# When the dense matrix of the second token tile is built: six units in it instead of seven, and an issue ratio of five gathers to four

## Chip, core and metric

The kernel runs on one core of a Trainium2 chip. The metric is the device time of one execution in microseconds (us); lower is better. Three runs of the kernel before gave 1784.56, 1786.32 and 1787.67 us, median 1786.32.

## What is computed

A decoder layer over 256 tokens of width 2048: attention and gated convolution, an output projection, a layer norm giving h, then a retrieval of single-neuron experts (PEER), then a second layer norm. The change lies wholly in PEER:

```python
q = (h @ w_query).reshape(B, S, 8, 2, 128)
s = einsum('bshcd,hckd->bshck', q, sub_keys)      # two lists of 128 keys per head
# top 16 of each list, top 16 of the 16x16 sums; eid = i1 * 128 + i2
g = softmax(best_s)
a = gelu(einsum('td,thkd->thk', h, expert_u[eid]))
y = einsum('thk,thkd->td', g * a, expert_v[eid])
```

Each of 256 tokens picks 16 experts in each of 8 heads out of 16384. Each pick reads one row of `expert_u` and one of `expert_v`, 2048 float32 each (8 KB).

## The kernel before

**Tiles and units.** The tokens form tile 0 and tile 1 of 128 tokens, one token per partition. A unit is one tile and one head: units 0 to 7 are tile 0, units 8 to 15 are tile 1. A unit has 16 picks, numbered m = 16 n + k. One indirect DMA of the GpSimd (POOL) queue brings one pick of all 128 tokens, a 128 x 2048 tile of 1 MB: `gather_u` (L525) into one of 8 `u_slot`s, `gather_v` (L542, L545) into one of 7 `v_slot`s.

**Four steps per pick.** (1) VectorE (DVE) multiplies the U rows by the tokens and sums (`dot`, L1760). (2) ScalarE (ACT) takes exp and gelu per unit (`unit`, made of `expo_gate` and `gelu_unit`), and DVE makes the coefficients (`gates_of`, L1766 to L1771, which counts `coef_ok`). (3) For V picks 0 to 143 TensorE (PE) adds the V rows, times diagonal matrices that ACT writes (`diagonals`), into PSUM (L974). (4) For V picks 144 to 255 DVE adds them into `xh` (`add_row`, L1795) after its last dot and after one scaling of `xh` (L1839).

**The dense part.** The last 40 x 128 = 5120 rows of `expert_v` (first key index 88 or more) are not gathered for units that use `bounds_check=ROWS - 1`: a pick in them moves nothing, and its coefficient in `gate` is made zero. They are instead multiplied as a dense product at the end: for each of 40 blocks f, 128 rows of `expert_v` are loaded by the SP queue (L429) into `u_slot` f % 6 and multiplied with a 128 x 128 coefficient matrix of tile 0 and one of tile 1 (`dense_mm`, L946, 8 matmuls issued as 2 passes each of 128 x 512 for each tile and block; tile 1 runs three blocks behind tile 0). The last unit, 15, is gathered whole (L545) and stands in no matrix.

**Building the matrix.** Per tile: PE transposes the ids and coefficients of its units (`pick_transposes`, L928; `PICKS` is the number of rows, 128 for tile 0 and 112 = 7 units for tile 1), ACT copies them (`picks_out`, L1307). Then for 16 groups b of 8 tokens: DVE makes two one-hot tables (`hot_rows`, L1783, L1785, L1788), PE multiplies them (`dense_rows`, L938, 16 passes), ACT copies the result into `dense0` or `dense1` (`dense_out`, L1316; L1319 and L1320). There are two buffers, so `hot_rows` b waits for `dense_rows` b - 2, and `dense_rows` b for `dense_out` b - 2.

**What sets the order.** Every engine's queue is written out by hand. POOL sends V picks in order and before V pick m as many U picks as `64 + (m + 1) * 4 // 3` (L555); at m = 144 all U picks left. A U gather waits for the dot eight before it, a V gather for the pick seven before it to be used. DVE's queue is the 256 dots; `HOT0_AT` and `HOT1_AT` say after which dot a `hot_rows` of tile 0 or 1 stands (192 to 233 for tile 0; 244 to 254 for groups 0 to 7 of tile 1, groups 8 to 15 behind the last dot). `gates_of(n - 1)` stands at k = 10 of unit n, for the last one at k = 2. PE's queue is V picks 0 to 143 with `dense_rows` of tile 0 before picks 97, 99, ... 127, the token tile's own product (L963) before pick 128, `pick_transposes(1)` before pick 132 and `dense_rows` of tile 1 groups 0 to 7 before picks 133 to 140, groups 8 to 15 behind pick 143, then `sum0` (L981) and the 40 blocks. SP's first six block loads wait for dots 248 to 253, the others for PE (`dense_used`). DVE takes the statistics of tile 0 before V pick 246, writes tile 0's result before pick 248 and adds PE's sum of tile 1 before pick 253 (L1847 to L1859).

Of the kernel before, what the change touches and what calls it, by code (L numbers as in the profile page):

```python
# [12 lines left out]
P = 128  # L13
# [15 lines left out]
NKEY = 128  # L29
TOPK = 16  # L30
NU = 16
RU = 8
RV = 7
AHEAD = 4
EARLY_V = 4
PH = 8
V0_PICKS = TOPK * PH
PE_PICKS = V0_PICKS + TOPK
RD = 6
FD = 40  # L40
FA = 24
ROWS = (NKEY - FD) * NKEY
LEAD = 3
G_TOK = 8
NG_T = P // G_TOK
PICKS = (P, P - TOPK)
IDS_AT = {(0, 4): 1, (8, 9): 10, (9, 1): 11, (9, 9): 12, (10, 1): 13, (10, 9): 14, (11, 1): 15}
IDS_AT.update({(n, 1): n + 1 for n in range(1, 9)})
HOT0_AT = {12 * TOPK + 11 * b // 4: b for b in range(NG_T)}
HOT1_AT = {15 * TOPK + 4 + 3 * b // 2: b for b in range(NG_T // 2)}  # L50
HTW = SEQ + 2
TCOL = (slice(0, P), slice(P + 2, SEQ + 2))
JOBS = [(0, (0,)), (1, (0,)), (0, (1,)), (1, (1,))] + [(h, (0, 1)) for h in range(2, PH)]
# [69 lines left out]
def build(nc, x, w_in, cmp_k_pos, cmp_k_w1, cmp_k_b1, cmp_k_w2, cmp_v_pos, cmp_v_w1, cmp_v_b1, cmp_v_w2,  # L123
# [133 lines left out]
    b_id = at("b_id", [P, 2, NU, TOPK], F32, o_lo + 2 * K)  # L257
    u_dot = at("u_dot", [P, NU, TOPK], F32, o_lo + 4 * K)
    gate = at("gate", [P, NU, TOPK], F32, o_lo + 5 * K)
# [182 lines left out]
    def _(pool):  # L442
# [86 lines left out]
        def gather_v(n, k):  # L529

            m = TOPK * n + k
            if m == 0:
                pool.wait_ge(S["wq_used"], 12)
            if m == EARLY_V:
                pool.wait_ge(S["wq_used"], 16)
            if RV <= m < PE_PICKS + RV:
                pool.wait_ge(S["v_used"], m - RV + 1)
            if m >= PE_PICKS + RV:
                pool.wait_ge(S["v_dve"], m - RV - PE_PICKS + 1)
            src = bass.IndirectOffsetOnAxis(ap=eid[:, n, k:k + 1], axis=0)  # L540
            if n < NU - 1:
                nc.gpsimd.indirect_dma_start(out=v_slot[m % RV][:, :], out_offset=None, in_=expert_v[0], in_offset=src,  # L542
                                             bounds_check=ROWS - 1, oob_is_err=False).then_inc(s_v[m % RV], 16)
            else:
                nc.gpsimd.indirect_dma_start(out=v_slot[m % RV][:, :], out_offset=None, in_=expert_v[0], in_offset=src  # L545
                                             ).then_inc(s_v[m % RV], 16)
# [5 lines left out]
                    gather_v(0, k)  # L552
        sent = TOPK * AHEAD
        for m in range(EARLY_V, TOPK * NU):
            while sent < min(TOPK * NU, TOPK * AHEAD + (m + 1) * 4 // 3):  # L555
                gather_u(sent // TOPK, sent % TOPK)
                sent += 1
            if m == PE_PICKS:
                while sent < TOPK * NU:
                    gather_u(sent // TOPK, sent % TOPK)  # L560
                    sent += 1
            gather_v(m // TOPK, m % TOPK)
# [3 lines left out]
    def _(pe):  # L566
# [354 lines left out]
        scores_of(len(JOBS) - 1)  # L921
        def pick_transposes(t):

            pe.wait_ge(S["coef_ok"], (PH, NU - 1)[t])
            n = PICKS[t]
            units = slice(PH * t, PH * t + n // TOPK)
            for i, src in enumerate((b_id[:, 0, units, :], b_id[:, 1, units, :], b_val[:, units, :])):
                ins = nc.tensor.transpose(bank[(2, 6)[t]][0:n, P * i:P * i + P], src.rearrange("p n k -> p (n k)"), ident[:, :])  # L928
            ins.then_inc(S["pick_mm"], 1)

        def dense_rows(t, b):

            g, n = NG_T * t + b, PICKS[t]
            pe.wait_ge(S["hot_ok"], g + 1)
            if g >= 2:
                pe.wait_ge(S["dense_ok"], g - 1)
            for i in range(G_TOK):
                ins = nc.tensor.matmul(bank[4 * t + g % 2][:, FD * i:FD * i + FD], hot2[0:n, g % 2, i, :], hot1[0:n, g % 2, i, :],  # L938
                                       start=True, stop=True, skip_group_check=True)
            ins.then_inc(S["dense_mm"], 1)  # L940
# [12 lines left out]
        for m in range(PE_PICKS):  # L953
            n, k = divmod(m, TOPK)
            if k == 0:
                pe.wait_ge(S["diag_ok"], n + 1)
            if m == 80:
                pick_transposes(0)
            if m >= 97 and m % 2 and m < V0_PICKS:
                dense_rows(0, (m - 97) // 2)  # L960
            if m == V0_PICKS:
                for q in range(4):
                    ins = nc.tensor.matmul(bank[4 + q][:, :], ident_a[:, :], xh[:, 0, 512 * q:512 * q + 512],  # L963
                                           start=False, stop=True)
                ins.then_inc(S["t0_part"], 1)
                pe.wait_ge(S["dense_ok"], NG_T)
            if m == V0_PICKS + 4:
                pe.wait_ge(S["part_ok"], 1)
                pick_transposes(1)
            if V0_PICKS + 5 <= m < V0_PICKS + 5 + NG_T // 2:  # L970
                dense_rows(1, m - V0_PICKS - 5)
            pe.wait_ge(s_v[m % RV], 16 * (m // RV + 1))
            for q in range(4):
                ins = nc.tensor.matmul(bank[(4 if n < PH else 0) + q][:, :], diag[:, n % 2, k, :],  # L974
                                       v_slot[m % RV][:, 512 * q:512 * q + 512], start=(m in (0, V0_PICKS)), stop=False)
            ins.then_inc(S["v_used"], 1)
        for b in range(NG_T // 2, NG_T):
            dense_rows(1, b)
        pe.wait_ge(S["dense_ok"], 2 * NG_T)
        for q in range(4):  # L980
# [10 lines left out]
    def _(act):  # L991
# [280 lines left out]
        def gelu_unit(n):  # L1272
            act.wait_ge(S["dots_done"], TOPK * (n + 1))
            nc.scalar.activation(u_dot[:, n, :], u_dot[:, n, :], ACT.Gelu_apprx_tanh).then_inc(S["gelu_ok"], 1)

        def diagonals(n):
            act.wait_ge(S["coef_ok"], n + 1)
            if n >= 2:
                act.wait_ge(S["v_used"], TOPK * (n - 1))
            for k in range(TOPK):  # L1280
                ins = nc.scalar.activation(diag[:, n % 2, k, :], ident[:, :], ACT.Copy, scale=gate[:, n, k:k + 1])
            ins.then_inc(S["diag_ok"], 1)
# [21 lines left out]
        def picks_out(t):  # L1304
            act.wait_ge(S["pick_mm"], t + 1)
            n = PICKS[t]
            nc.scalar.activation(pickT[0:n, t, :, :].rearrange("p a t -> p (a t)"), bank[(2, 6)[t]][0:n, 0:3 * P], ACT.Copy  # L1307
                                 ).then_inc(S["pick_ok"], 1)
# [14 lines left out]
        def unit(n):  # L1323
            expo_gate(n)
            gelu_unit(n)
# [13 lines left out]
        diagonals(5)  # L1339
        unit(9)  # L1340
        diagonals(6)
        unit(10)
        picks_out(0)
        unit(11)
        diagonals(7)
        for b in range(NG_T):
            if b in (6, 12):
                unit(11 + b // 6)
            if b == 10:
                diagonals(8)  # L1350
            dense_out(0, b)
        act.wait_ge(S["t0_part"], 1)
        for q in range(4):
            ins = nc.scalar.activation(sum0[:, 512 * q:512 * q + 512], bank[4 + q][:, :], ACT.Copy)
        ins.then_inc(S["part_ok"], 1)
        unit(14)
        expo_gate(15)
        picks_out(1)
        for b in range(NG_T):
            if b == NG_T // 2:  # L1360
                gelu_unit(15)
            dense_out(1, b)
        for t in range(2):
            root(t)

# [2 lines left out]
    def _(dve):  # L1368
# [394 lines left out]
        def gates_of(n):  # L1763

            dve.wait_ge(S["exp_ok"], n + 1)
            V.reciprocal(g_inv[:, n:n + 1], g_sum[:, n:n + 1])  # L1766
            dve.wait_ge(S["gelu_ok"], n + 1)
            dve.drain()
            V.scalar_tensor_tensor(b_val[:, n, :], u_dot[:, n, :], g_inv[:, n:n + 1], b_val[:, n, :], ALU.mult, ALU.mult)
            dve.drain()  # L1770
            V.scalar_tensor_tensor(gate[:, n, :], b_id[:, 0, n, :], float(NKEY - FD) if n < NU - 1 else float(NKEY),  # L1771
                                   b_val[:, n, :], ALU.is_lt, ALU.mult).then_inc(S["coef_ok"], 1)

        def hot_rows(t, b):
# [40 lines left out]
        for n in range(NU):  # L1815
            for k in range(TOPK):
                dot(n, k)
                if (n, k) == (0, 1):
                    dve.wait_ge(S["t1_mm"], 4)
                    last_row(1)  # L1820
                    mean_of(1)
                if (n, k) in IDS_AT:
                    ids(IDS_AT[n, k])
                if (n, k) == (0, 8):
                    inverse_std(1)
                    dve.wait_ge(S["yt_mm"], 9)
                    for half in range(2):
                        token_major(1, half)
                    dve.drain().then_inc(S["h1_ok"], 1)
                if n and k == (10 if n < NU - 1 else 2):  # L1830
                    gates_of(n - 1)
                m = TOPK * n + k
                if m in HOT0_AT:
                    hot_rows(0, HOT0_AT[m])
                if m in HOT1_AT:
                    hot_rows(1, HOT1_AT[m])
        for b in range(NG_T // 2, NG_T):
            hot_rows(1, b)
        V.tensor_scalar(xh[:, 1, :], xh[:, 1, :], ALPHA, None, ALU.mult)  # L1839
        dve.drain()  # L1840
# [56 lines left out]
```

## Time and profile before

| | us |
|---|---|
| median of three runs | 1786.32 |
| the profiled execution, its own time | 1785.23 |
| its span, first to last instruction | 1783.5 |
| PE busy | 1515.2 (85%) |
| DVE busy | 1361.8 (76%) |
| POOL busy | 963.2 (54%) |
| ACT busy | 391.1 (22%) |

The sixteen DMA engines are near 100% busy from about 45% of the span on, but for a hole in slices 31 and 32 of 40. Times in the rows count from the span's start. A row of the stretches gives for each engine the busy time and number of instructions, then the granted TensorE clock as a share of 2.4 GHz, the busy share of the DMA engines and their GB/s.

### The profile page before, as it was taken

Reading aid. Unit: us, or ns where it says so; the run is one execution under the profiler, and the core shown is the slowest. Engines: PE = TensorE matmul, PEld = TensorE weight load, DVE = VectorE, ACT = ScalarE, POOL = GpSimd, SP = SyncE. Lnnn points to the kernel's source line nnn. Section 1 sums busy time; section 2 is a strip of 40 time slices with the busy share of each in tenths; the row PEclk is TensorE's granted clock in tenths of the full one; section 3 lists DMA queues with packets and bytes.
Section 4 is the critical chain, followed back from the end, with each engine's and each line's share of the span. In section 5 each row is a group of like instructions: output and inputs, shape, how many; then the busy total and the mean of one; then the engine's idle time right before and its main releaser. Section 6 shows DMA issues by size and latency. Waiting matters only on the chain.

```text
span 1783.5 us, 16886 instructions
## 1 busy us (share of the span) xinstructions
PE 1515.2 (85%) x6164; PEld 950.5 (53%) x6164; DVE 1361.8 (76%) x1915; ACT 391.1 (22%) x824; POOL 963.2 (54%) x591
## 2 busy tenths in 40 slices
PE   8999999999989709888777778798977899999970
PEld 7988999988668504333333333344534564444430
DVE  6666646676879998776788888677867487788788
ACT  5665464664101211102010110101210110000000
POOL 3210000000456677878776767888886147578761
PEclk9999999999989859898999988999997879999995
DMA  9876444474999999999999999999999639999994
GB/s 313 288 257 198 120 141 142 143 250 162 377 380 421 389 425 418 420 425 426 420 425 425 417 425 418 422 420 412 415 406 418 235 118 401 405 404 408 414 414 179
DMA packets 159380, 610.87 MB, mean 343 GB/s; under 512 B 21467, under 2 KB 74807, under 8 KB 97255
## 3 DMA queue, kind: packets, MB, share of 16 engines
q0 software_dynamic: 79232, 480.80, 66.2%
q1 hardware_dynamic: 80064, 128.99, 20.3%
q8 instruction: 48, 0.79, 0.2%
q14 instruction: 36, 0.29, 0.0%
HBM read 683.42 MB, written 2.10 MB: 384 GB/s over the span
## 4 chain that ended last, share of the span: by engine, by line
PE 33%; DMA 22%; DVE 18%; POOL 15%; issue 9%; DVEq 2%; ACT 1%; SPq 0%; POOLq 0%; ACTq 0%
PE psum_all L587 13%; DMA v_slot<-in_expert_v_dram,eid 13%; POOL v_slot L542 9%; DVE u_slot L1760 8%; DMA u_slot<-in_expert_u_dram,eid 8%; PE psum_all L974 7%; POOL u_slot L525 6%; PE psum_all L727 4%; DVE xh L1795 3%; PE psum_all L938 2%; PE psum_all L752 1%; PE psum_all L708 1%; PE psum_all L612 1%; PE psum_all L614 1%; PE psum_all L674 0%
## 5 line engine op out<-in xcount | busy, mean ns | idle before, releaser
L974 PE MATMUL psum_all<-v_slot,diag 128*128 128x512 f32 x1152 | 570.9, 650 | 152.6 <-DMA v_slot<-in_expert_v_dram,eid 104.4
L1760 DVE SCALAR_TENSOR_TENSOR u_slot<-u_slot,xh 128x2048 f32<-128x2048 f32 x256 | 577.7, 2289 | 149.6 <-DMA u_slot<-in_expert_u_dram,eid 148.4
L525 POOL DMA_INDIRECT u_slot<-in_expert_u_dram,eid x256 | 445.4, 1740 | 267.1 <-DVE u_slot L1760 99.7
L542 POOL DMA_INDIRECT v_slot<-in_expert_v_dram,eid x240 | 452.8, 1887 | 176.1 <-issue 63.6
L974 PEld LDWEIGHTS psum_all<-v_slot,diag 128*128 128x128 f32 x1152 | 231.7, 208 | 471.5 <-issue 271.0
L1795 DVE SCALAR_TENSOR_TENSOR xh<-v_slot,gate,xh 128x2048 f32<-128x2048 f32 x112 | 263.5, 2353 | 52.5 <-DMA v_slot<-in_expert_v_dram,eid 44.5
L1378 DVE TENSOR_TENSOR w_lo<-w_ring,w_hi 128x512 fp32r<-128x512 f32 x240 | 156.6, 688 | 77.6 <-ACT w_hi L1010 74.5
L587 PE MATMUL psum_all<-act_hi,w_hi 128*128 128x256 f32 x640 | 185.0, 289 | 1.2 <-DVE w_lo L1378 1.2
L587 PE MATMUL psum_all<-act_lo,w_hi 128*128 128x256 f32 x640 | 180.8, 282 | 0.0
L587 PE MATMUL psum_all<-act_hi,w_lo 128*128 128x256 f32 x640 | 180.2, 282 | 0.0
L1010 ACT ACTIVATE w_hi<-w_ring 128x512 fp32r<-128x512 f32 x240 | 139.3, 622 | 42.3 <-PE psum_all L587 41.2
L946 PE MATMUL psum_all<-u_slot,dense 128*128 128x512 f32 x320 | 143.4, 592 | 0.0
L587 PEld LDWEIGHTS psum_all<-act_hi,w_hi 128*128 128x128 f32 x640 | 121.2, 189 | 13.7 <-issue 4.1
L752 PE MATMUL psum_all<-hT,wq_ring 128*128 128x258 f32 (+2 forms) x640 | 120.8, 349 | 8.6 <-DMA wq_ring<-in_w_query_dram 8.2
L587 PEld LDWEIGHTS psum_all<-act_lo,w_hi 128*128 128x128 f32 x640 | 121.2, 189 | 2.7 <-issue 0.5
L587 PEld LDWEIGHTS psum_all<-act_hi,w_lo 128*128 128x128 f32 x640 | 121.0, 189 | 0.0
L752 PEld LDWEIGHTS psum_all<-hT,wq_ring 128*128 128x128 f32 x640 | 106.0, 198 | 24.0 <-DMA wq_ring<-in_w_query_dram 8.6
L513 POOL DMA_DIRECT2D skeys<-in_sub_keys_dram x1 | 1.2, 1165 | 197.1 <-PE psum_all L587 197.1
L946 PEld LDWEIGHTS psum_all<-u_slot,dense 128*128 128x128 f32 x320 | 60.8, 190 | 76.5 <-issue 76.5
L938 PEld LDWEIGHTS psum_all<-hot,hot 128*128 128x128 f32 (+1 forms) x512 | 76.0, 233 | 29.6 <-DVE hot L1788 20.7
L938 PE MATMUL psum_all<-hot,hot 128*128 128x40 f32 (+1 forms) x512 | 75.5, 318 | 15.7 <-DVE hot L1788 15.7
L946 PE MATMUL psum_all<-u_slot,dense1a 128*128 128x512 f32 x192 | 86.3, 592 | 0.0
(283 smaller groups left out, 1462.7 us busy)
## 6 DMA issues: line engine op xcount, KB each, us to landing
w_ring<-in_w_in_dram SPq DMA_DIRECT2D x88, 512.0 KB, 5.0
u_slot<-in_expert_v_dram SPq DMA_DIRECT2D x40, 1024.0 KB, 8.7
wo_ring<-in_w_out_dram SPq DMA_DIRECT2D x32, 512.0 KB, 5.0
wq_ring<-in_w_query_dram SPq DMA_DIRECT2D x32, 512.0 KB, 10.0
w_ring<-in_cmp_k_w_dram POOLq DMA_DIRECT2D x16, 512.0 KB, 6.0
w_ring<-in_cmp_v_w_dram POOLq DMA_DIRECT2D x16, 512.0 KB, 4.4
u_slot<-in_expert_u_dram,eid POOLq DMA_INDIRECT x256
v_slot<-in_expert_v_dram,eid POOLq DMA_INDIRECT x256
```

What stands on the lines that cost most here:

```text
L525: nc.gpsimd.indirect_dma_start(out=u_slot[m % RU][:, :], out_offset=None, in_=expert_u[0], in_offset=bass.IndirectOffsetOnAxis(ap=eid[:, n ...
L542: nc.gpsimd.indirect_dma_start(out=v_slot[m % RV][:, :], out_offset=None, in_=expert_v[0], in_offset=src, bounds_check=ROWS - 1, oob_is_er ...
L587: ins = nc.tensor.matmul(o, st, mv, start=(k == 0 and b == 0 and i == 0), stop=(k == KC - 1 and i == 2), skip_group_check=True)
L727: ins = nc.tensor.matmul(bank[acc + b][:, :], st[:, k, half], mv[:, n % RING, :], start=(i == 0 and m == 0), stop=(i == KC - 1 and m == 2))
L752: ins = nc.tensor.matmul(bank[QBANK[h % 2] + c][:, cols], wq_ring[j % 2][:, k // 4, k % 4, 256 * (h % 2) + 128 * c:256 * (h % 2) + 128 * c ...
L938: ins = nc.tensor.matmul(bank[4 * t + g % 2][:, FD * i:FD * i + FD], hot2[0:n, g % 2, i, :], hot1[0:n, g % 2, i, :], start=True, stop=True ...
L946: ins = nc.tensor.matmul(bank[(4 if t == 0 else 0) + q][:, :], src, u_slot[f % RD][:, 512 * q:512 * q + 512], start=False, stop=(f == FD - 1))
L974: ins = nc.tensor.matmul(bank[(4 if n < PH else 0) + q][:, :], diag[:, n % 2, k, :], v_slot[m % RV][:, 512 * q:512 * q + 512], start=(m in ...
L1010: nc.scalar.activation(w_hi[:, n % RING, :], raw_item(n), ACT.Copy).then_inc(S["hi_done"], 1)
L1378: V.tensor_tensor(w_lo[:, n % RING, :], raw_item(n), w_hi[:, n % RING, :].bitcast(F32), ALU.subtract).then_inc(S["lo_done"], 1)
L1760: V.scalar_tensor_tensor(u_slot[m % RU][:, :], u_slot[m % RU][:, :], 1.0, xh[:, n // PH, :], ALU.mult, ALU.mult, accum_out=u_dot[:, n, k:k ...
L1795: V.scalar_tensor_tensor(xh[:, 1, :], v_slot[m % RV][:, :], gate[:, n, k:k + 1], xh[:, 1, :], ALU.mult, ALU.add)
```

## The change

The matrix of tile 1 holds units 8 to 13 (`PICKS` 96); units 14 and 15 are gathered whole, with no bounds check, and their coefficients are not cut. POOL sends U picks by `64 + (m + 1) * 5 // 4`. The `hot_rows` of tile 0 stand after dots 180 to 217, all sixteen of tile 1 after dots 229 to 255; PE's `dense_rows` of tile 0 before picks 93 to 123, those of tile 1 groups 0 to 7 before picks 133 to 142 by a list. The coefficients of unit 13 are made at dot 226. ACT's queue is reordered to fit.

```diff
+ROWS1_AT = [133, 134, 136, 137, 138, 140, 141, 142]
-PICKS = (P, P - TOPK)
+PICKS = (P, P - 2 * TOPK)
-HOT0_AT = {12 * TOPK + 11 * b // 4: b for b in range(NG_T)}
-HOT1_AT = {15 * TOPK + 4 + 3 * b // 2: b for b in range(NG_T // 2)}
+HOT0_AT = {180 + 5 * b // 2: b for b in range(NG_T)}
+HOT1_AT = {14 * TOPK + 5 + 7 * b // 4: b for b in range(NG_T)}
...
-            if n < NU - 1:
+            if n < NU - 2:
                 nc.gpsimd.indirect_dma_start(out=v_slot[m % RV][:, :], out_offset=None, in_=expert_v[0], in_offset=src,
                                              bounds_check=ROWS - 1, oob_is_err=False).then_inc(s_v[m % RV], 16)
...
-            while sent < min(TOPK * NU, TOPK * AHEAD + (m + 1) * 4 // 3):
+            while sent < min(TOPK * NU, TOPK * AHEAD + (m + 1) * 5 // 4):
...
-            pe.wait_ge(S["coef_ok"], (PH, NU - 1)[t])
+            pe.wait_ge(S["coef_ok"], (PH, NU - 2)[t])
...
-            if m >= 97 and m % 2 and m < V0_PICKS:
-                dense_rows(0, (m - 97) // 2)
+            if m % 2 and 93 <= m < 93 + 2 * NG_T:
+                dense_rows(0, (m - 93) // 2)
...
-            if V0_PICKS + 5 <= m < V0_PICKS + 5 + NG_T // 2:
-                dense_rows(1, m - V0_PICKS - 5)
+            if m in ROWS1_AT:
+                dense_rows(1, ROWS1_AT.index(m))
...
         diagonals(6)
+        picks_out(0)
         unit(10)
-        picks_out(0)
-        unit(11)
-        diagonals(7)
         for b in range(NG_T):
-            if b in (6, 12):
-                unit(11 + b // 6)
-            if b == 10:
+            if b == 2:
+                diagonals(7)
+            if b in (5, 11):
+                unit(11 + b // 11)
+            if b == 11:
                 diagonals(8)
             dense_out(0, b)
...
-        unit(14)
+        unit(13)
+        expo_gate(14)
         expo_gate(15)
         picks_out(1)
         for b in range(NG_T):
-            if b == NG_T // 2:
-                gelu_unit(15)
+            if b == 7:
+                gelu_unit(14)
             dense_out(1, b)
+        gelu_unit(15)
...
-            V.scalar_tensor_tensor(gate[:, n, :], b_id[:, 0, n, :], float(NKEY - FD) if n < NU - 1 else float(NKEY),
+            V.scalar_tensor_tensor(gate[:, n, :], b_id[:, 0, n, :], float(NKEY - FD) if n < NU - 2 else float(NKEY),
...
-                if n and k == (10 if n < NU - 1 else 2):
+                if n and k == (10 if n < NU - 2 else 2):
                     gates_of(n - 1)
...
-        for b in range(NG_T // 2, NG_T):
+        for b in range(len(HOT1_AT), NG_T):
             hot_rows(1, b)
```

## Rows read from the trace of the kernel before

**Rows 1.** The page: GB/s in 40 slices of the span.

```profile
GB/s 313 288 257 198 120 141 142 143 250 162 377 380 421 389 425 418 420 425 426 420 425 425 417 425 418 422 420 412 415 406 418 235 118 401 405 404 408 414 414 179
```

**Rows 2.** Busy time of each engine by stretch, granted clock, DMA share, GB/s.

```profile
1150.00:1340.00 190.00, 164.27 (x548) 87.03 (x547) 145.63 (x154) 32.00 (x62) 164.10 (x86) 0.94 1.01 414
1345.00:1400.00 55.00, 42.86 (x158) 26.56 (x157) 37.90 (x42) 4.32 (x12) 24.55 (x16) 0.81 0.99 406
1400.00:1450.00 50.00, 49.01 (x196) 37.06 (x196) 29.72 (x35) 10.03 (x23) 7.51 (x6) 0.70 0.24 77
1450.00:1480.00 30.00, 30.00 (x68) 13.16 (x67) 28.57 (x13) 0.00 (x0) 24.97 (x12) 0.95 0.81 266
1500.00:1700.00 200.00, 200.00 (x467) 88.54 (x466) 161.32 (x69) 0.00 (x0) 145.84 (x69) 1.00 1.00 409
1757.00:1783.50 26.50, 0.00 (x0) 0.00 (x0) 22.14 (x20) 0.29 (x1) 0.00 (x0) 0.50 0.17 67
```

**Rows 3.** Timeline of DVE: from dot 244 to the first added row, cut.

```profile
1345.15 2.29 DVE L1760 SCALAR_TENSOR_TENSOR u_slot<-u_slot,xh 128x2048 f32<-128x2048 f32 x1 [2.20 <-DMA u_slot<-in_expert_u_dram,eid]
...
1403.82 2.29 DVE L1760 SCALAR_TENSOR_TENSOR u_slot<-u_slot,xh 128x2048 f32<-128x2048 f32 x1 [0.26 <-DMA u_slot<-in_expert_u_dram,eid]
...
1424.20 0.49 DVE L1783 TENSOR_TENSOR hot<-iota_row,pickT 112x320 f32<-112x320 f32 x1 [13.33 <-PE psum_all L938]
...
1430.12 0.49 DVE L1783 TENSOR_TENSOR hot<-iota_row,pickT 112x320 f32<-112x320 f32 x1 [1.61 <-PE psum_all L938]
...
1442.47 1.22 DVE L1839 TENSOR_SCALAR xh<-xh 128x2048 f32<-128x2048 f32 x1
1443.77 39.42 DVE L1795 SCALAR_TENSOR_TENSOR xh<-v_slot,gate,xh 128x2048 f32<-128x2048 f32 x16
```

**Rows 4.** Timeline of PE: the stop before pick 132, and the build's end.

```profile
1340.89 0.65 PE L928 MATMUL psum_all<-ident,b_id 128*112 128x128 f32 x2 [10.76 <-DVE gate L1771]
...
1408.47 13.98 PE L974 MATMUL psum_all<-v_slot,diag 128*128 128x512 f32 x32
...
1426.45 20.70 PE L938 MATMUL psum_all<-hot,hot 112*128 112x40 f32 x96 [0.17 <-DVE hot L1788]
1447.96 6.07 PE L981 MATMUL psum_all<-sum,ident 128*128 128x512 f32 x8 [0.81 <-ACT dense1b L1320]
...
1714.81 13.90 PE L946 MATMUL psum_all<-u_slot,dense1b 128*128 128x512 f32 x32
```

**Rows 5.** Timeline of DVE near the end, cut.

```profile
1716.11 19.68 DVE L1795 SCALAR_TENSOR_TENSOR xh<-v_slot,gate,xh 128x2048 f32<-128x2048 f32 x8 [0.50 <-DMA v_slot<-in_expert_v_dram,eid]
...
1761.39 2.29 DVE L1859 TENSOR_TENSOR xh<-xh,psum_all 128x2048 f32<-128x2048 f32 x1
```

**Rows 6.** DMA queues and issues from 1450 us to the end.

```profile
q0 software_dynamic: 15120, 82.10, 61.9%
...
v_slot<-in_expert_v_dram,eid POOLq DMA_INDIRECT x104
```

**Rows 7.** Timeline of DVE: dots back to back around one hot_rows of tile 0.

```profile
1240.44 2.29 DVE L1760 SCALAR_TENSOR_TENSOR u_slot<-u_slot,xh 128x2048 f32<-128x2048 f32 x1
1242.65 0.49 DVE L1783 TENSOR_TENSOR hot<-iota_row,pickT 128x320 f32<-128x320 f32 x1
...
1244.76 2.28 DVE L1760 SCALAR_TENSOR_TENSOR u_slot<-u_slot,xh 128x2048 f32<-128x2048 f32 x1
```

**Rows 8.** Timeline of POOL: the last U gather; a V gather beside DVE's adds.

```profile
1372.25 0.94 POOL L525 DMA_INDIRECT u_slot<-in_expert_u_dram,eid  x1 [0.30 <-issue]
...
1457.20 2.16 POOL L542 DMA_INDIRECT v_slot<-in_expert_v_dram,eid  x1 [0.30 <-issue]
```

**Rows 9.** Timeline of PE: one group of tile 0 between picks, in step.

```profile
1297.12 1.87 PE L938 MATMUL psum_all<-hot,hot 128*128 128x40 f32 x16
1298.83 7.11 PE L974 MATMUL psum_all<-v_slot,diag 128*128 128x512 f32 x16
1305.78 1.87 PE L938 MATMUL psum_all<-hot,hot 128*128 128x40 f32 x16
```

More of the change, by code:

```diff
@@ L976, in _ @@
             ins.then_inc(S["v_used"], 1)
-        for b in range(NG_T // 2, NG_T):
+        for b in range(8, NG_T):
             dense_rows(1, b)
@@ L1836, in _ @@
                     hot_rows(1, HOT1_AT[m])
-        for b in range(NG_T // 2, NG_T):
+        for b in range(len(HOT1_AT), NG_T):
             hot_rows(1, b)
```

## The prediction

> **What bounds the kernel now.** I began with the transfer rate over the span. From slice 12 on it stays near 400 to 425 GB/s, the rate of full DMA engines, but for two slices at 235 and 118 [rows 1]. By stretches [rows 2] the engines are full until 1400 us (share 0.99, 406 GB/s), then carry 77 GB/s for 50 us and 266 GB/s for 30 us, and are full again to the end. Against 409 GB/s the hole is (409 - 77) x 50 = 16.6 MB and (409 - 266) x 30 = 4.3 MB: 20.9 MB or 51 us of lost transfer. Everything beside it is transfer-bound; PE and DVE have idle time there.
>
> What makes the hole is in the two timelines. DVE's last dot ends at 1406.04, but its first added row, which frees the first `v_slot`, comes at 1443.77 [rows 3]. Between lie groups 8 to 15 of tile 1's matrix: DVE waits 13.33 us at one of them, since PE has four V picks to do first (1408.47 to 1422.45), and the rest goes at PE's half clock, six groups in 20.70 us [rows 4]. PE was late because it had stood 10.76 us before pick 132 for the coefficients of unit 14, made at dot 242 [rows 4]. With 7 V slots and 6 block buffers full, nothing else can be transferred.
>
> **The change, step by step.** *Where dot 244 falls.* V picks cost less than U picks because of the bounds check. Window from 1450 us: POOL's queue moved 82.10 MB with 104 gathers issued in it and one (pick 151, issued at 1447) landing in it [rows 6]; 16 are whole (1.049 MB from the shape), so the other 89 moved 65.3 MB, 0.734 MB each. Before, U pick 244 goes out behind V picks 0 to 134, now behind 0 to 143 (from the two issue formulas). Nine more V picks are 6.6 MB, at 406 GB/s [rows 2] 16.2 us. Dot 244 began at 1345.15 with its data just landed [rows 3]; now 1361.4, if the engines stay full.
>
> *From dot 244 to the first added row.* The last 12 U gathers follow each other. Their dots and the seven `hot_rows` after dots 244, 246, 248, 250, 251, 253, 255 are DVE work in a row: a dot takes 2.21 us start to start, a group 2.11 [rows 7], so 26.5 + 14.8 = 41.3 us. Transfers need 12 x 1.049 / 0.406 = 31 us, so DVE is the limit; from dot 248 on, block loads and V picks 144 to 150 fill the engines again. Then the scaling, 1442.47 to 1443.77, 1.3 us [rows 3]. First added row: 1361.4 + 41.3 + 1.3 = 1404.0.
>
> *What can be late in between.* Three handshakes are new, and the trace has none of them at these places. Dot 226 needs the gelu of unit 13, which on ACT stands behind the `sum0` copies and so behind PE's pick 127. Dot 229 needs `picks_out(1)`, behind PE's pick 131, which is sent right after U pick 228. Dot 242 needs the gelu of unit 14, behind `dense_out` 6. Dots 229 to 243 hold 15 dots, nine groups and one `gates_of` of three instructions on 16 columns, for which I put 0.7 us: 33.2 + 19.0 + 0.7 = 53 us of DVE against 15 U and 12 V picks, 24.5 MB or 60 us. So 7 us of waits are hidden there. Below: nothing is lost. Above: one wait like the longest there is, 13.33 us [rows 3]. I take 3 us seen at the end, nearer to the lower bound, since PE goes in step with the picks when no coefficient holds it (a group each 8.65 us for two picks [rows 9], where transfers bring two picks in 10 us: five U and four V picks are 8.2 MB, 20 us). First added row at 1407.0, 36.8 us earlier than before. Queued behind any wait of DVE are the `u_slot`s, hence POOL's U gathers and, POOL being in order, the V gathers.
>
> *What PE does then.* The last `dense_rows` follows DVE's last group by one half-clock group (3.4 us) and the ACT copies (0.9). PE starts the dense products as before some 4 us behind DVE's first add and needs the same time: first `sum0` at 1447.96, end at 1728.7, 281 us [rows 4]. It moves by the same 37 us. Before, it ended 33 us ahead of the use of its sum at 1761.39 [rows 5], so nothing waits for it.
>
> *Unit 14 whole.* 16 x (1.049 - 0.734) = 5.0 MB more in the last stretch. It is transfer-bound at 409 GB/s [rows 2]: 12.3 us. From 1716.11 DVE runs without waiting [rows 5]; at the same distance from its first add it will be 5.0 / 1.049 = 4.8 picks further back, 4.8 x 2.46 = 11.8 us (eight adds took 19.68), so both ways of counting agree. The 0.734 MB holds elsewhere: in 1150 to 1340 POOL issued 86 gathers, some 49 U and 37 V by the ratio; 414 x 190 = 78.7 MB less 51.4 leaves 0.74 each [rows 2]. A single unit may differ; I allow a third of what is dropped either way, 8 to 16 us. A page of the Trainium skill would charge more: "DMA: Bandwidth & Descriptors", section "Where 436 GB/s comes from", puts the HBM limit of one core near 358 GB/s. By that rule 5.0 MB would be 14.0 us. The trace disagrees for this one-core kernel, with 409 GB/s over 200 us [rows 2], and the sum does not use it.
>
> *Edits at no cost.* Sixteen groups of tile 0 go 12 dots earlier and 0.25 dot closer; DVE was busy 145.63 of 190 us there, PE 164.27 [rows 2]; per five dots DVE now has 11.1 + 4.2 us in 20 us of transfers. If that cover went, each group would cost 2.1 us. Matrix rows 96 instead of 112 change no duration (L1783 takes 0.49 us on 112 and on 128 partitions [rows 3, 7]). The changed cut of the coefficients is the same instruction. ACT's reordering is covered by its idle time (busy 32 of 190 us [rows 2]). SP's queue is untouched; its first six loads follow the dots. The ratio 5:4 moves no bytes in total; it puts V picks earlier and U picks later, and so sends PE a pick each 5.0 us instead of each 5.2. POOL issues 12 U gathers in a row; one took 0.94 us free and a V gather 2.16 beside DVE's adds [rows 8], so 12 x (2.2 + 0.3) = 30 us, under DVE's 41.
>
> *Sum.* -36.8 + 12.3 = -24.5 us. Span 1783.5 - 24.5 = 1759.0; with the 1.7 us around it (1785.23 less 1783.5), 1760.7 us. The profiled execution stood 1.1 us under the median of the runs, which I don't correct for. Forecast 1761.
>
> **The rivals.** *A, DVE waits for PE in the build.* PE works at clock 0.81 in 1345 to 1400 [rows 2], and a group at half clock takes 20.70 / 6 = 3.45 us [rows 4]. Ten picks and eight groups need 48 us at full clock (3.43 and 1.71 [rows 9]) and 60 at 0.81, against 50 us of transfers. PE falls 10 us behind, its V slots hide it from POOL, but not from DVE's groups from 10 on, which stand behind pick 143. For it: the clock falls in just such mixed work. Against it: before, much of the fall came with the stop for the coefficients. Price 10 to 14 us: 1773. Chance 0.20.
>
> *B, the hole closes further.* From dot 244 on there remain 11 U picks (11.5 MB), 80 cut and 32 whole V picks (58.7 + 33.6), 40 blocks (41.9) and two rows (2.1): 147.8 MB, at 406 GB/s 364 us. If the engines never run dry, the last V pick lands at 1725.4 instead of about 1757, behind which the engines carry little [rows 2], and with the 26.5 us that follow the span is 1752: 1753 to 1754 us. For it: by dot 248 everything waits to be sent. Against: seven slots did not keep up in the first 36 us after 1443.77 (266 GB/s). Chance 0.15.
>
> *C, slower: the groups among the dots hold the gathers.* Place: dots 229 to 243, nine groups that wait for PE's `dense_rows` two before, itself behind a V pick that POOL sends only when DVE frees `u_slot`s. If each waited one V pitch (5 us), 45 us less the 7 hidden would stand against the gain: +38 - 24.5 gives 1799. It decides from 24.5 + 7 = 31.5 us of waits, 3.5 us a group; before, all waits of this kind but the long one were 1.61 us or less [rows 3]. Against: before group b = 0 to 7 PE's pick is sent at least two U picks before the dot that needs it. Chance 0.06.
>
> *D, the change does not do what it says.* The last group stands behind dot 255, so the matrix is ready with U's end and not ahead of it; if ACT's gelu of unit 14 or the late half-clock groups push the end 20 us further, 4 us are left: 1781. Chance 0.05.
>
> The forecast's own case has 0.54.
>
> **How the numbers follow.** The likeliest case gives 1761, with the unit's share (8 to 16 us) and waits from 0 to 7 us 1754 to 1769. The range takes in A and B: 1749 to 1776. C and D lie above it, with the worst of A. Under 0.2% (3.6 us, about what can be told from no change here) either way: 0.04, from D and the edge of A. Slower by over 0.2%: 0.07, C and a mishap of its kind. Faster: 0.89.
>
> **What would show it.** In the new profile: no 10.76 us stop at L928; dot 244 near 1361; the last dot near 1400; only the group of dot 255 behind the last dot; first L1795 at 1404 to 1411; the stretch of 77 GB/s gone, with the lowest 50 us over 300 GB/s; POOL's queue 5 MB larger; `sum0` near 1411; whole picks at DVE waiting for transfers for 16 picks longer. Wrong would be: a first add after 1420 (A, C), DVE waiting for PE at L1783 for over 7 us in total before dot 243, a second hole after the first add, or a last stretch grown by other than 8 to 16 us.

## The result, and the profile after

The changed kernel takes 1756.5 us (median of four runs, 1754.4 to 1757.1) against 1785.4 us of the kernel before beside it (1784.6 to 1787.7): 28.9 us less, ratio 0.983 with interval 0.9815 to 0.9846. The profiled execution has a span of 1754.7 us against 1783.5, 28.8 us less. The forecast was 1761 us in a range of 1749 to 1776.

First the page of the changed kernel, GB/s in 40 slices and the line of POOL's DMA queue (packets, MB, share).

```profile
GB/s 318 273 267 217 120 145 123 142 213 219 312 378 420 386 425 423 409 425 425 423 425 423 416 425 419 415 410 418 420 419 425 382 287 414 403 410 404 426 428 197
...
q0 software_dynamic: 79232, 485.32, 67.6%
```

The slices of 235 and 118 GB/s [rows 1] are now 382 and 287: the hole has become a dip. POOL's queue carries 485.32 MB; before, its line on the page said 480.80. Gathering unit 14 whole therefore moves 4.52 MB more, not 5.0.

Busy time by stretch, with the columns of [rows 2]: two stretches shown before, two parts of the dip, 36 us from the first added row on, and the 235 us after them.

```profile
1345.00:1400.00 55.00, 42.22 (x188) 31.08 (x186) 51.07 (x59) 8.02 (x20) 33.62 (x18) 0.75 0.96 390
1400.00:1450.00 50.00, 45.06 (x115) 23.77 (x116) 47.68 (x30) 2.74 (x6) 32.89 (x16) 0.83 0.83 304
...
1370.00:1380.00 10.00, 5.33 (x37) 5.21 (x36) 9.58 (x11) 1.47 (x4) 4.23 (x3) 0.63 0.81 297
1380.00:1390.00 10.00, 4.62 (x21) 4.32 (x20) 9.85 (x12) 1.44 (x4) 9.09 (x4) 0.50 0.93 373
...
1408.93:1444.93 36.00, 35.18 (x83) 16.85 (x83) 34.32 (x15) 2.02 (x4) 27.19 (x13) 0.89 0.76 258
1444.93:1680.00 235.07, 235.07 (x549) 104.07 (x548) 180.48 (x81) 0.00 (x0) 157.35 (x79) 1.00 1.00 412
```

In 1345 to 1400 DVE is busy 51.07 of 55 us, where it had 37.90 [rows 2]: the groups have filled its idle time. In 1400 to 1450 the engines carry 304 GB/s instead of 77.

The timeline of DVE says where the time came from. It shows dot 229 with the first group of tile 1 behind it, dots 243 and 244 with a group between them, then the last group, the scaling and the first added rows.

```profile
1303.28 2.29 DVE L1763 SCALAR_TENSOR_TENSOR u_slot<-u_slot,xh 128x2048 f32<-128x2048 f32 x1 [2.32 <-DMA u_slot<-in_expert_u_dram,eid]
1307.12 0.49 DVE L1786 TENSOR_TENSOR hot<-iota_row,pickT 96x320 f32<-96x320 f32 x1 [1.54 <-ACT pickT L1308]
...
1361.71 2.28 DVE L1763 SCALAR_TENSOR_TENSOR u_slot<-u_slot,xh 128x2048 f32<-128x2048 f32 x1
1363.92 0.48 DVE L1786 TENSOR_TENSOR hot<-iota_row,pickT 96x320 f32<-96x320 f32 x1
...
1366.02 2.28 DVE L1763 SCALAR_TENSOR_TENSOR u_slot<-u_slot,xh 128x2048 f32<-128x2048 f32 x1
...
1405.52 0.48 DVE L1786 TENSOR_TENSOR hot<-iota_row,pickT 96x320 f32<-96x320 f32 x1
...
1407.63 1.22 DVE L1842 TENSOR_SCALAR xh<-xh 128x2048 f32<-128x2048 f32 x1
1408.93 39.42 DVE L1798 SCALAR_TENSOR_TENSOR xh<-v_slot,gate,xh 128x2048 f32<-128x2048 f32 x16
```

The first added row comes at 1408.93 instead of 1443.77 [rows 3], 34.8 us earlier. From it to the end of the span are 345.8 us, against 1783.5 - 1443.77 = 339.7 before: 6.0 us more. 34.8 - 6.0 = 28.8 us is the whole difference of the two spans.

What the two stretches waited for, from the waits by engine and line (us in total, times, longest), DVE alone up to 1409 us, and of the kernel before up to 1444 us. After:

```profile
DVE u_slot L1763 <- DMA u_slot<-in_expert_u_dram,eid: 10.1, 8, 2.6
DVE hot L1786 <- ACT pickT L1308: 1.5, 1, 1.5
```

Before:

```profile
DVE u_slot L1760 <- DMA u_slot<-in_expert_u_dram,eid: 33.3, 17, 6.6
DVE hot L1783 <- PE psum_all L938: 19.0, 6, 13.3
```

DVE's 19 us of waiting for PE are gone, with no wait of that kind in their place. Its waits for U gathers fell too, from 33.3 to 10.1 us: groups are now built in time that it had spent waiting for them. PE's timeline shows why DVE no longer waits for it: `pick_transposes(1)` follows the picks without the stop of 10.76 us [rows 4], and PE waits for DVE's last groups instead, which it can afford.

```profile
1306.07 0.38 PE L929 MATMUL psum_all<-ident,b_id 128*96 128x128 f32 x2
...
1407.76 3.63 PE L939 MATMUL psum_all<-hot,hot 96*128 96x40 f32 x16 [2.89 <-DVE hot L1791]
1412.21 6.02 PE L982 MATMUL psum_all<-sum,ident 128*128 128x512 f32 x8 [0.82 <-ACT dense1b L1321]
```

### The profile page after: what moved, and what is told of

It reads as the page before. It is cut to its first block, busy times and chain, and to the rows that moved or that the text cites. A ratio compares the mean times of both kernels' runs of the same rounds, so it can differ in the third digit from the quotient of the medians.

```text
span 1754.7 us, 16868 instructions
## 1 busy us (share of the span) xinstructions
PE 1496.5 (85%) x6164; PEld 942.6 (54%) x6164; DVE 1359.9 (77%) x1915; ACT 388.2 (22%) x822; POOL 957.1 (55%) x591
## 3 DMA queue, kind: packets, MB, share of 16 engines
q0 software_dynamic: 79232, 485.32, 67.6%
## 4 chain that ended last, share of the span: by engine, by line
PE 32%; DVE 19%; DMA 19%; POOL 17%; issue 11%; DVEq 2%; ACT 1%; SPq 0%; POOLq 0%; ACTq 0%
PE psum_all L588 13%; DVE u_slot L1763 9%; DMA v_slot<-in_expert_v_dram,eid 9%; POOL v_slot L543 9%; DMA u_slot<-in_expert_u_dram,eid 9%; POOL u_slot L526 6%; PE psum_all L975 6%; PE psum_all L728 4%; DVE xh L1798 3%; PE psum_all L753 1%; POOL v_slot L546 1%; PE psum_all L709 1%; PE psum_all L939 1%; PE psum_all L613 1%; PE psum_all L615 1%
## 5 line engine op out<-in xcount | busy, mean ns | idle before, releaser
L975 PE MATMUL psum_all<-v_slot,diag 128*128 128x512 f32 x1152 | 553.7, 635 | 131.5 <-DMA v_slot<-in_expert_v_dram,eid 84.0
L526 POOL DMA_INDIRECT u_slot<-in_expert_u_dram,eid x256 | 434.8, 1699 | 283.1 <-DVE u_slot L1763 109.9
L543 POOL DMA_INDIRECT v_slot<-in_expert_v_dram,eid x224 | 427.5, 1909 | 114.2 <-issue 62.5
L975 PEld LDWEIGHTS psum_all<-v_slot,diag 128*128 128x128 f32 x1152 | 225.4, 202 | 438.7 <-issue 261.6
L753 PE MATMUL psum_all<-hT,wq_ring 128*128 128x258 f32 (+2 forms) x640 | 119.5, 346 | 10.1 <-DMA wq_ring<-in_w_query_dram 9.6
L939 PE MATMUL psum_all<-hot,hot 128*128 128x40 f32 (+1 forms) x512 | 75.5, 315 | 28.8 <-DVE hot L1791 28.8
L939 PEld LDWEIGHTS psum_all<-hot,hot 128*128 128x128 f32 (+1 forms) x512 | 75.2, 229 | 43.4 <-DVE hot L1791 34.8
```

Of the source, the lines that this page charges most:

```text
L526: nc.gpsimd.indirect_dma_start(out=u_slot[m % RU][:, :], out_offset=None, in_=expert_u[0], in_offset=bass.IndirectOffsetOnAxis(ap=eid[:, n ...
L753: ins = nc.tensor.matmul(bank[QBANK[h % 2] + c][:, cols], wq_ring[j % 2][:, k // 4, k % 4, 256 * (h % 2) + 128 * c:256 * (h % 2) + 128 * c ...
```

## The experiments

### What unit 14 whole costs

I had put 12.3 us for it; the last stretch grew by 6.0. Two theories: A, the term was mis-sized; B, the term was right for its bytes and another 5 us were won in the same stretch. First the changed kernel with the bounds check on unit 14's gathers again; the sum then leaves out unit 14's picks in the last 5120 rows.

```diff
-            if n < NU - 2:
+            if n < NU - 1:
                 nc.gpsimd.indirect_dma_start(...)
```

> The changed kernel, but unit 14's 16 V gathers keep the bounds check (its picks in the last 5120 rows are left out of the sum, so only the time counts). It prices unit 14 whole inside the changed kernel. Theory A, the term was mis-sized: POOL's queue grew by 4.5 MB and these picks fall where DVE ends the run anyway, so they cost the 6.0 us by which the stretch from the first add to the end grew: 1750 us. Theory B, the term was nearly right (4.5 MB at 413 GB/s, 10.9 us) and another 5 us were won in the same stretch, by a shallower dip after the first add (258 GB/s for 36 us against 219): 1745 to 1746 us, and the stretch from first add to end 335 us instead of 345.8.

1750.7 us (1749.9 to 1752.5). The 16 gathers cost 5.8 us inside the changed kernel, as theory A has it. From its first added row (1407.81) to the end of the span are 340.5 us, where B asked for 335. Second, from the other side, the kernel before with unit 14 whole.

```diff
-PICKS = (P, P - TOPK)
+PICKS = (P, P - 2 * TOPK)
-            if n < NU - 1:
+            if n < NU - 2:
                 nc.gpsimd.indirect_dma_start(...)
-            ... float(NKEY - FD) if n < NU - 1 else float(NKEY),
+            ... float(NKEY - FD) if n < NU - 2 else float(NKEY),
```

> The kernel before with unit 14 gathered whole and 96 rows in the matrix, all places and the ratio as before. Theory A: 6 us slower, 1791 us. Theory B: 10 to 12 us slower, 1796 us. In both the first add stays at 1443 to 1446 us, since PE still stops for unit 14's coefficients; if the first add moves, the smaller matrix itself was worth something.

1793.0 us against 1786.6, ratio 1.0036 (1.0023 to 1.0048): 6.4 us. The first added row stood at 1443.58, unmoved, PE's stop still at 10.77 us. So the smaller matrix did not move the first added row, and theory A holds on both sides. B falls.

But 4.52 MB at 412 GB/s are 11.0 us. Where are the other five? The line `n < NU - 2` says which units keep the bounds check. Two runs change the number of whole units in both directions: the changed kernel with `n < NU - 3` (unit 13 whole too) and with `n < NU` (units 14 and 15 both cut, their picks in the last 5120 rows left out of the sum).

> The changed kernel with unit 13's V gathers whole as well; its picks in the last 5120 rows have coefficient zero, so only the bytes change, some 4.5 to 5 MB. Theory T, the tail has a slack: with unit 14 cut the engines carried 378, 391, 397 and 321 GB/s in the last 40 us of gathers and had room for two whole picks, which unit 14 used up (428, 427, 428, 419 GB/s in the changed kernel). Then a second unit finds no room and costs its full transfer time, 10 to 12 us: 1767 us. Theory U, a unit costs 6 us wherever it stands, because only DVE's 2.46 us a pick count: 1762 us.

1771.2 us (1768.3 to 1771.7), 14.7 above the changed kernel. POOL's queue carried 491.18 MB, so the bounds check had saved 5.86 MB in unit 13. That is 14.2 us at 412 GB/s: the full price. My figure of 10 to 12 us rested on a guess of the bytes.

> The changed kernel with the bounds check on all V gathers: rows of units 14 and 15 beyond the check are left out of the sum, only the time counts. Against the run with unit 14 alone cut (1750.7 us). Theory T: the last stretch is then DVE's, which already ran without a wait from 1678 us on, so cutting unit 15 too gains 0 to 2 us: 1749 to 1751 us, and the engines carry still less at the end. Theory U: 6 us less, 1745 us. Bytes alone: 11 us less, 1740 us.

1749.7 us (1749.5 to 1751.0), 1.0 below the run with unit 14 cut, though it moved 6.06 MB less (474.74 against 480.80 MB). The two ranges overlap, so this 1.0 us can't be told from nothing. Busy time in 1680 to 1720 us, the same 40 us of four kernels; each fence is one kernel. Both units cut:

```profile
1680.00:1720.00 40.00, 11.69 (x28) 4.88 (x26) 37.79 (x22) 0.29 (x1) 24.50 (x12) 0.69 0.71 242
```

Unit 14 cut:

```profile
1680.00:1720.00 40.00, 11.39 (x27) 4.75 (x25) 37.79 (x22) 0.30 (x1) 25.55 (x12) 0.69 0.94 372
```

The changed kernel:

```profile
1680.00:1720.00 40.00, 12.89 (x31) 5.37 (x29) 37.48 (x21) 0.29 (x1) 25.91 (x13) 0.71 1.01 426
```

Unit 13 whole too:

```profile
1680.00:1720.00 40.00, 11.89 (x28) 4.94 (x26) 37.76 (x19) 0.00 (x0) 32.40 (x16) 0.69 1.01 427
```

DVE is busy 37.5 to 37.8 us of 40 in all four: it limits this tail. The DMA engines go from 242 over 372 to 426 GB/s and stay there. The first whole unit finds room in them and costs about 1 us; the second finds less and costs 5.8; the third finds none and pays 14.7.

What the second pays can be read from where DVE's last unbroken run begins. Unit 14 cut, then the changed kernel:

```profile
1678.43 22.12 DVE L1798 SCALAR_TENSOR_TENSOR xh<-v_slot,gate,xh 128x2048 f32<-128x2048 f32 x9 [1.09 <-DMA v_slot<-in_expert_v_dram,eid]
```

```profile
1682.43 24.60 DVE L1798 SCALAR_TENSOR_TENSOR xh<-v_slot,gate,xh 128x2048 f32<-128x2048 f32 x10 [0.42 <-DMA v_slot<-in_expert_v_dram,eid]
```

Ten more adds follow in both, behind the first tile's statistics. So the run begins 4.0 us later with one pick of 2.46 us more: 6.5 us, where the two spans differ by 6.4 (1754.7 - 1748.3), 1.1 of it an earlier first added row. With unit 13 whole too, the run begins at 1681.63 with 25 picks left instead of 20: 12.3 - 0.8 = 11.5 us, where the spans differ by 11.6. (The profiled execution of that kernel is the fastest of its four.)

An estimate by room comes out near as well, but it was made after the fact and hangs on the stretch chosen: (426 - 372) x 40 = 2.2 MB fit into the second unit's room, and the rest, (4.52 - 2.2) / 1.049 = 2.2 picks at 2.46 us, is 5.4 us. Of the theories T (the tail has slack) fits; U (6 us each) and the count by bytes alone both fail. The runs make the units whole in one order only, the last unit first, so they do not separate how many units are whole from where in the queue a unit stands.

### What the places of the groups and the ratio are worth

Here groups 8 to 15 go back behind the last dot, all else as in the changed kernel.

```diff
-HOT1_AT = {14 * TOPK + 5 + 7 * b // 4: b for b in range(NG_T)}
+HOT1_AT = {14 * TOPK + 5 + 7 * b // 4: b for b in range(NG_T // 2)}
```

> The changed kernel with groups 8 to 15 of tile 1 behind the last dot, as before; the rest unchanged. If the place of these groups is what counts: dots 244 to 255 become transfer-bound and end near 1397, then eight groups at 3.45 us each and the scaling: first add near 1426, 17 us later than 1408.9, and 1771 to 1774 us. If the stop of PE for unit 14's coefficients was the main loss and the place of the last groups little: first add before 1415, under 1763 us.

1777.4 us, first added row at 1430.29: the place of these eight groups is worth 20.9 us. It came 4 us later than I put: the dots ended 7 us later (1403.9, expected 1397), the eight groups took 25.1 us instead of 27.6. The loss lies in the last five dots; two of them from the timeline of DVE in this run:

```profile
1386.96 2.29 DVE L1763 SCALAR_TENSOR_TENSOR u_slot<-u_slot,xh 128x2048 f32<-128x2048 f32 x1 [2.59 <-DMA u_slot<-in_expert_u_dram,eid]
1391.88 2.29 DVE L1763 SCALAR_TENSOR_TENSOR u_slot<-u_slot,xh 128x2048 f32<-128x2048 f32 x1 [2.62 <-DMA u_slot<-in_expert_u_dram,eid]
```

4.9 us from dot to dot is two transfers of 1.049 MB at 427 GB/s: beside each U gather the engines bring something else of its size. That it is SP's block loads, which start with dot 248, is my reading; no run took them away. This kernel still beats the second run by 15.6 us. The earlier start of groups 0 to 7, the ratio, the places of tile 0's groups and ACT's order share that, and no run separates them.

The ratio alone can't be set back. At 4:3, V pick 131 goes out behind U pick 239, which waits for dot 231, while DVE would stand behind dot 229 for the transposes behind pick 131. So each engine would wait for the other for good. That is read from the queues, and was not tried. Instead the groups were moved to where 4:3 allows them, with tile 0's groups, the coefficients of unit 13 and most of ACT's order as before (not shown here):

```diff
-HOT1_AT = {14 * TOPK + 5 + 7 * b // 4: b for b in range(NG_T)}
+HOT1_AT = {15 * TOPK + b: b for b in range(NG_T)}
-            while sent < min(TOPK * NU, TOPK * AHEAD + (m + 1) * 5 // 4):
+            while sent < min(TOPK * NU, TOPK * AHEAD + (m + 1) * 4 // 3):
-ROWS1_AT = [133, 134, 136, 137, 138, 140, 141, 142]
+ROWS1_AT = [133, 134, 135, 136, 137, 138, 139, 140, 141, 142, 143]
...
-            if b == 7:
+            if b == 0:
                 gelu_unit(14)
```

> Unit 14 whole, ratio 4:3 as before, tile 0's groups and ACT's order as before, all sixteen groups of tile 1 behind dots 240 to 255, PE's groups 0 to 10 before picks 133 to 143, coefficients of unit 13 at dot 234. DVE work from dot 240 (near 1329) is 16 x (2.21 + 2.11) = 69 us. If DVE never waits for PE: first add near 1404, 1752 us. If the V picks, sent later than at 5:4, hold the groups (group 12 at dot 252 stands behind pick 142, sent after U pick 253), DVE waits about 10 us: first add near 1414, 1762 us. If the ratio itself is what matters, over 1770 us.

1771.5 us, first added row at 1423.91. DVE waited 10.1 us for transfers in 1300 to 1430 us, as in the changed kernel, but the waits for PE came back; from the waits of DVE in 1300 to 1430 us:

```profile
DVE hot L1785 <- PE psum_all L939: 22.2, 10, 9.5
```

The longest, 9.50 us, ends at 1411.89, and just before it PE itself had stood 5.63 us for the transfer of its last V pick. My reading is that 5:4 moves the V picks, and with them PE, far enough ahead of DVE that all sixteen groups fit between the dots. Ratio and places changed together here: together they are worth 15 us, and what the ratio is worth alone stays open.

### What is left

After the change there are two dips, before and behind the first added row (297 and 373 GB/s in 1370 to 1390 us, then 258 over 36 us). Three edits aim at them. `LEAD` is the number of blocks by which tile 1's products run behind tile 0's. With 0 the two products of a block follow each other, which by the count of products ahead of it frees the first block buffer 10 us earlier:

```diff
-LEAD = 3
+LEAD = 0
```

> The changed kernel with LEAD 0: tile 1's product of a block follows tile 0's at once instead of three blocks later, so PE frees the first block buffer 6.9 us after it starts instead of 17 us, and the block loads resume 10 us earlier, into the dip behind the first add (220 to 320 GB/s from 1415 to 1445). If that dip is lost transfer which the end pays for: some 1.5 MB earlier, 3 to 4 us faster, 1753 us. If the end is set by DVE and its V slots, or the loads only displace V gathers: no change, 1756 us. Slower (over 1758) if DVE then waits for the statistics of tile 0, whose sum comes only 3.4 us before PE's end instead of 13.7.

1754.1 us, but with runs from 1751.5 to 1758.0, on both sides of those of the changed kernel: inconclusive by itself. The engines carried 295 GB/s instead of 258 in the 36 us behind the first added row, and DVE did not wait for tile 0's statistics. The second edit sets the groups denser, one behind every 1.5 dots:

```diff
-ROWS1_AT = [133, 134, 136, 137, 138, 140, 141, 142]
+ROWS1_AT = [133, 134, 136, 137, 138, 139, 140, 141, 142, 143]
-HOT1_AT = {14 * TOPK + 5 + 7 * b // 4: b for b in range(NG_T)}
+HOT1_AT = {14 * TOPK + 5 + 3 * b // 2: b for b in range(NG_T)}
...
-        for b in range(8, NG_T):
+        for b in range(len(ROWS1_AT), NG_T):
...
+        sp.wait_ge(S["dots_done"], TOPK * NU)
         for row, src in ((ln2g_sb, ln2_g), (ln2b_sb, ln2_b)):
```

> The changed kernel with tile 1's groups behind every 1.5 dots (229 to 251) instead of 1.75 (229 to 255), PE's first ten before picks 133 to 143, and one wait on SP so that the ln2 rows still load after the last dot. DVE waited 7.8 us for transfers between dots 229 and 243, so three groups (6.3 us) fit there for nothing. If DVE's work from dot 244 on sets the first add: first add 4 to 6 us earlier. The end gains it only as far as the engines were idle before the first add (297 and 373 GB/s in 1370 to 1390, 1.5 MB or 4 us): 1752 to 1754 us. If transfers alone set the end: 1756 us.

1751.8 us (1750.1 to 1754.5), 4.7 below the changed kernel; the first added row stands at 1405.94, 3.0 us earlier, and the rest was won behind it. Both edits:

> Both edits of the two runs beside it. If their gains are separate pieces of lost transfer (dip before and dip behind the first add), they add: 1748 to 1751 us. If both only move the same idle time, no better than the better one.

1748.0 us (1746.4 to 1748.8), 8.5 below the changed kernel, where the two alone gave 2.4 and 4.7. The gains do not hide each other; that they add exactly can't be said, since the first was inconclusive. The last piece is the two rows of the second layer norm (`ln2`), 2.1 MB, loaded behind the sixth block instead of behind the last (first on the changed kernel, then on top of both edits):

```diff
             sp.dma_start(u_slot[f % RD][:, :], ...).then_inc(s_d[f % RD], 16)
+            if f == RD - 1:
+                sp.wait_ge(S["dots_done"], TOPK * NU)
+                for row, src in ((ln2g_sb, ln2_g), (ln2b_sb, ln2_b)):
+                    sp.dma_start(row[:, :], ...).then_inc(S["s_ln2row"], 16)
-        for row, src in ((ln2g_sb, ln2_g), (ln2b_sb, ln2_b)):
-            sp.dma_start(row[:, :], ...).then_inc(S["s_ln2row"], 16)
```

> The changed kernel with the ln2 rows loaded behind the sixth block, nothing else (one more wait for the last dot on SP). Up to 5 us for 2.1 MB moved from the full stretch to the dip: 1751 to 1753 us. If the loads delay block 6 or V picks that DVE needs at once: 1756 us or more.

1750.0 us, ratio 0.9796 (0.9783 to 0.9809): 6.5 us less for moving 2.1 MB out of the full stretch. 2.4 us of it is an earlier first added row (1406.51), for which I have no cause; part may be scatter, since four kernels whose program is the same up to there (the changed one, those with unit 14, with both units cut and with unit 13 whole) have it between 1407.81 and 1408.93. Beside the changed kernel's 258 GB/s, this one carries in the same 36 us:

```profile
1408.90:1444.90 36.00, 35.19 (x77) 15.49 (x77) 32.71 (x14) 2.02 (x4) 29.27 (x14) 0.92 0.90 326
```

> The run with denser groups and LEAD 0 (1748.0 us), and the two ln2 rows (2.1 MB) loaded behind the sixth block instead of behind the fortieth. They then fall into the dip behind the first add (260 GB/s over 36 us), and not into the stretch where DVE waits for V picks. If the end pays for bytes moved in that full stretch: 2.1 MB at 413 GB/s, up to 5 us: 1743 to 1745 us. If the dip has no room left after LEAD 0: 1748 us.

1747.1 us (1745.5 to 1748.4), ratio to the kernel before 0.9781 (0.9767 to 0.9794): the fastest median, but not told apart from 1748.0. In its 36 us from 1404.6 on the engines are full:

```profile
1404.60:1440.60 36.00, 36.00 (x83) 15.92 (x82) 27.87 (x14) 1.50 (x2) 19.96 (x11) 0.97 1.01 410
```

In the run without the early loads this stretch already carried 373 GB/s, so there was little room left to use. What remains is the stretch from 1676 us to the end, where DVE is busy 62 of 68 us.

## Why the prediction was right, and where it was off

**The hole and its cause: right.** The 51 us of lost transfer lay where the first view put them, and the groups behind the last dot made them: with eight of them put back the first added row falls 21 us behind.

**Where dot 244 falls: 4.6 us off.** 1366.02, forecast 1361.4. From dot 229 (1303.28) to dot 244 passed 62.7 us; I had 53 us of DVE work against 60 of transfers and called 7 us hidden. DVE had its work and 9.3 us of waits, 7.8 of them for U gathers that came at uneven distances. That makes 2.7 us more than the 60; counted back by the same 60 us, dot 229 was 1.9 us late already. Most of the 7 us did stay hidden.

**From dot 244 to the first added row: right for DVE, not for the engines.** 41.6 us to the scaling, forecast 41.3, in a row without a wait for a transfer; scaling 1.3. But block loads and V picks did not keep the engines full at once: they carried 297 GB/s in 1370 to 1380, 373 in the next 10 us, and the first block load starts at 1381.74.

**The handshakes: 1.5 us, forecast 3 with 0 to 13.** Only `picks_out(1)` was waited for, and its 1.5 us are part of the 4.6 above. That the first added row came at 1408.9, so near to 1407.0, is partly luck: the 3 us that I had set aside for handshakes covered most of the 4.6 us, of which only 1.5 were a handshake.

**PE: right.** `sum0` at 1412.21, 3.3 us behind the first added row (4.2 before), and the last product ends 280.7 us later, at 1692.9 (forecast 281); DVE never waited for its sum.

**Unit 14 whole: the step that failed.** "16 x (1.049 - 0.734) = 5.0 MB more ... 12.3 us", and "4.8 picks further back ... so both ways of counting agree". It was 4.52 MB and 6.0 us, below the 8 to 16 us that I allowed; a last stretch grown by other than that was one of my own signs of being wrong. At the point where DVE's last unbroken run begins, 1682.43, 273.5 us behind the first add, 20 picks were left; before, 18 were left 272.3 us behind it. That is two picks back, not 4.8: 2 x 2.46 + 1.2 = 6.1 us. Both of my ways counted bytes, so their agreement proved nothing. The step took the last stretch as transfer-bound to its end, and its tail was DVE's. The rows showed that DVE ran without a wait from 1716.11 [rows 5], and I used that to price a pick at 2.46 us, but not to ask whether the engines had room there. They had: with unit 14 cut they carried 372 GB/s over the 40 us that the changed kernel fills with 426.

**The net:** -34.8 + 6.0 against -36.8 + 12.3. Two errors of opposite sign, 2.0 and 6.3 us, and the larger one made the result better than forecast. That the sum ended only 4.5 us off is partly luck, since one error took 2.0 us off the other.

**The rivals.** A asked for DVE waiting for PE: none, though the clock in 1345 to 1400 was 0.75 of full, below the 0.81 that A assumed. The picks and groups on PE went through in time for DVE all the same. C needed 31 us of waits at the groups; they were zero. B was nearer than its chance of 0.15 suggests in time (1753 to 1754), but not by its mechanism: the engines did not stay full, the two dips remained. D did not happen: the build did end with U's end, and that was enough. The run at 4:3 shows what waits for PE cost when they do come, though not from A's cause: 22 us of waits beside 15 us of time.

**The HBM rule** (the Trainium skill, "DMA: Bandwidth & Descriptors", section "Where 436 GB/s comes from", some 358 GB/s a core) would have made unit 14 dearer. The trace disagrees with it: this core carried 412 GB/s over 235 us and 426 over 40.

## What to carry to other kernels

When a stage is moved to fill a hole, the queue orders that let it move are part of the change: here the new places of the groups needed PE's picks to be sent ahead of them, and at 4:3, with the places that ratio allows, DVE waited 22 us for PE. Price extra bytes by who limits the stretch in which they are consumed, and ask what the engines still carry there: the same kind of edit cost some 1, 5.8 and 14.7 us for the first, second and third unit (6.06, 4.52 and 5.86 MB). Small loads with no hurry belong in a dip, not behind the last large one: moving two rows gave 6.5 us on the changed kernel, and nothing that could be measured once the dips were nearly full.

## What was not expected of the hardware

A gather on POOL takes longer beside DVE's dots. Four of the last seven V gathers before the first added row, and the two dots beside the second of them:

```profile
1382.83 1.30 POOL L543 DMA_INDIRECT v_slot<-in_expert_v_dram,eid  x1 [0.30 <-issue]
1384.44 4.67 POOL L543 DMA_INDIRECT v_slot<-in_expert_v_dram,eid  x1 [0.30 <-issue]
1389.42 1.23 POOL L543 DMA_INDIRECT v_slot<-in_expert_v_dram,eid  x1 [0.30 <-issue]
1390.95 2.46 POOL L543 DMA_INDIRECT v_slot<-in_expert_v_dram,eid  x1 [0.30 <-issue]
```

```profile
1383.74 2.28 DVE L1763 SCALAR_TENSOR_TENSOR u_slot<-u_slot,xh 128x2048 f32<-128x2048 f32 x1
...
1385.95 2.28 DVE L1763 SCALAR_TENSOR_TENSOR u_slot<-u_slot,xh 128x2048 f32<-128x2048 f32 x1
```

The longest take 4.67 us, against 0.94 free and 2.16 beside the adds [rows 8]. The timelines say what the length hangs on. The gather of 1384.44 ends 0.9 us behind the second dot. From 1290 to 1401 us, 20 gathers start while a dot runs, and each ends 0.8 to 0.9 us behind that dot's end, or behind the next dot's where two follow without a gap; the 24 that start beside no dot take 0.94 to 1.56 us. It is as if such a gather began its work only when the dot is done. It cost nothing here, but twelve in a row at the longest length would have been 60 us against DVE's 41, and my estimate of 2.2 us had no room for it. The Trainium skill, "SBUF — State Buffer", section "Who interferes with whom", says that a DVE instruction with two SBUF inputs contends with a GpSimd instruction that reads SBUF; the dots, groups and adds all have two, so the trace agrees with it, though no run here separates the cause.

The packets of POOL's queue are 79232 in every kernel, whether it carries 474.74 or 491.18 MB: a row that the bounds check drops still counts as a packet, but its bytes and their time are saved, as the 5.86 MB and 14.7 us of unit 13 show.
